# Moving the key products and the gain of an HGRN2 stage from VectorE and ScalarE to GpSimd

## The chip, the core and the metric

The kernel runs on one core of one Trainium2 chip. The metric is the device time of one launch in microseconds (us). A core has five engines with instruction streams of their own: PE (TensorE, matrix products), DVE (VectorE), ACT (ScalarE), POOL (GpSimd) and SP (SyncE, which here only starts transfers). They meet only at semaphores.

## The reference

A program of two blocks on 256 rows of width 1024: a first block with three attention branches and a feed-forward part, then two layers, one with an HGRN2 mixer and a feed-forward part, one with differential attention and a mixture of eight experts. The change touches the HGRN2 mixer alone:

```python
def hgrn2_mixer(h, w_in, lb_logits, norm_g, w_out, layer):
    q, f, i, g = jnp.split(h @ w_in, 4, axis=-1)
    lb = jnp.cumsum(jax.nn.softmax(lb_logits, axis=0), axis=0)[layer]
    forget = lb + (1.0 - lb) * jax.nn.sigmoid(f)
    log_f = jnp.log(forget)
    k = 1.0 - forget
    q = jax.nn.silu(q)
    v = i
    ...
        cum = jnp.cumsum(lf, axis=2)
        rel = jnp.where(tri, cum[:, :, :, None, :] - cum[:, :, None, :, :], -jnp.inf)
        scores = jnp.einsum('bhtd,bhsd,bhtsd->bhts', qc, kc, jnp.exp(rel))
    ...
    o = rms_norm_2(o, norm_g) * jax.nn.sigmoid(g).reshape(b, s, nh, dk)
    return o.reshape(b, s, D_MODEL) @ w_out
```

There are 8 heads of width 128. `norm_g` (`hg_norm_g_2`) is one gain for each of the 128 columns of a head, the same for all heads.

## The kernel before

All matrix products of the projections are done with each operand split into a high and a low part (three matmuls for one). Weights come by SP's queue into a ring; ACT writes the high part of each quarter of a weight tile (L1255, "a piece"), DVE the low part (L1864, the split), and PE uses them. Both run a few pieces ahead of PE and may write over a piece only when PE has used it.

The HGRN2 scores are computed by levels. Level i, from 0 to 8, pairs queries in the second half of each stretch of 2b positions with keys in its first half, b = 128, 64, 32, 16, 8, 4, 2, 1, and level 8 is the diagonal. For each level:

- DVE subtracts the cumulated log at the middle of each stretch (`level_differences`, L2244 or L2247, result in DD);
- ACT takes the exponentials of both halves into EE (`level_exps`, L1542 and L1543), and may do so only when queries and keys of the level before are done, since EE is written over;
- DVE multiplies the second halves of the queries QQ into QS (`level_queries`, L2257) and the first halves of the keys KK into KS (`level_keys`, L2266), when PE has read QS and KS of the level before;
- PE computes the products of all heads (`level`, L885), 16 matmuls for level 0 and 32 for each other, when both are there;
- the result goes from PSUM into the score matrix STT: by ACT for levels 0 and 1 (`level_copy`), by DVE under a mask from level 2 on (`level_place`, L2276, four predicated copies).

There is one QS, one KS, one EE and one DD. The order is written out by hand: the levels lie between the quarters q of four projections, hg0, hg1 (the gate), hv0, hv1 (the values), level i behind the quarter that LEVEL_AT gives, so that PE has two quarters of a projection between two levels:

```python
                    if (n, q) in LEVEL_AT:
                        i = LEVEL_AT[n, q]
                        if i + 1 < 8:
                            level_differences(i + 1)
                        if i >= 2:
                            level_place(i)
                        if i + 1 < 8:
                            level_queries(i + 1)
                            level_keys(i + 1)
```

The gate is tanh(x/2) on ACT (L1563) and then 0.5 t + 0.5 on DVE (`gate_rows2`, L2283), into GN, rows by columns. After the levels the scores are multiplied by the values, ACT squares the result, DVE sums (L2318), POOL takes the inverse root (L2758), DVE multiplies by the root (L2327) and by the gate (L2330). PE turns the result into columns (`columns("ho", ...)`), and there the gain is a number for each partition: ACT writes the high part times VT's column V_HN (L1273) and DVE the low part with the same column (L1892). That column comes by a 0.5 KB load of SP's into VS and a turn on PE, with all other column vectors.

POOL sets buffers to zero ahead of the stage, computes KK (L2848) and has no other work between 527 and 617 us. In other stages it multiplies and adds rows of 128x512 (L2780, L2782, L2838).

Of the kernel before, what the change touches and what calls it, by code (L numbers as in the profile page):

```python
# [54 lines left out]
V_MIX, V_MEM, V_FFN, V_LNG, V_LNB, V_QF, V_KF, V_QC, V_KC, V_LB, V_HN = 0, 8, 16, 24, 56, 88, 89, 90, 91, 92, 116  # L55
# [67 lines left out]
def build(nc, I, table, out):  # L123
    ctx = ExitStack()
    with ctx:
# [18 lines left out]
        NG = sb("NG", [128, 128])  # L144
# [65 lines left out]
        s_gth, s_gg, s_osq, s_od = (sem(n) for n in ("s_gth", "s_gg", "s_osq", "s_od"))  # L210
# [8 lines left out]
        T = {}  # L219
# [118 lines left out]
        VECTORS = [(V_FFN, "g_ffn", 8), (V_LNG, "ln_g_2", 32), (V_LNB, "ln_b_2", 32), (V_LB, "hg_lb_2", 24), (V_HN, "hg_norm_g_2", 1), (V_QC, "g_q_mem", 1), (V_KC, "g_k_mem", 1)]  # L338
# [80 lines left out]
        def pe_program(e):  # L419
# [262 lines left out]
            pe.wait_ge(s_vec, 16 * 11)  # L682
# [554 lines left out]
        def act_program(e):  # L1237
# [26 lines left out]
            def column_halves(name, scale=None, tts=(0, 1), halves=(0, 1), one=None):  # L1264
                for tt in tts:
                    a.wait_ge(*T["xfree", name, tt])
                    for half in halves:
                        j = 2 * tt + half
                        a.wait_ge(*banks.full["cols", name, j])
                        ps = PS[banks_of[name][j]].rearrange("p (a n) -> p a n", a=4)  # L1270
                        x = XH[:, 4 * half:4 * half + 4, 128 * tt:128 * tt + 128]
                        if one is not None:
                            e.activation(x, ps, ACT.Copy, scale=VT[:, one:one + 1]).then_inc(s_colh, 1)  # L1273
                        elif scale is None:
# [324 lines left out]
            column_halves("ho", one=V_HN)  # L1599
# [253 lines left out]
        def dve_program(e):  # L1853
# [29 lines left out]
            def column_lows(name, scale=None, tts=(0, 1), halves=(0, 1), one=None):  # L1883
                for tt in tts:
                    for half in halves:
# [5 lines left out]
                        if one is not None:  # L1891
                            e.scalar_tensor_tensor(out=l2, in0=ps, scalar=VT[:, one:one + 1], in1=h2.bitcast(F32), op0=ALU.mult, op1=ALU.subtract).then_inc(s_cols, 1)  # L1892
                        elif scale is None:
# [32 lines left out]
            def unit_rows(n):  # L1926
                nh = HEADS[n]
                for tt in range(2):
# [55 lines left out]
            def forget(stage):  # L1984
                if stage == 0:
# [3 lines left out]
                    v.wait_ge(s_bc, 16 * 7)  # L1989
# [80 lines left out]
            v.wait_ge(s_bc, 16 * 7)  # L2070
# [188 lines left out]
            def level_keys(i):  # L2259
                ev, kv, ksv = (flat(x).rearrange("p (y x b) -> p y x b", x=2, b=LEVELS[i]) for x in (EE, KK, KS))  # L2260
                v.wait_ge(s_ee, i + 1)
                v.wait_ge(s_set, 3)
                v.wait_ge(s_kk, 1)
                if i:
                    v.wait_ge(*T["level", i - 1])
                e.tensor_tensor(ksv[:, :, 0, :], kv[:, :, 0, :], ev[:, :, 0, :], ALU.mult).then_inc(s_ks, 1)  # L2266

# [31 lines left out]
            level_keys(0)  # L2299
            for n in ("hg0", "hg1", "hv0", "hv1"):  # L2300
                for q in range(4):
# [3 lines left out]
                    if (n, q) in LEVEL_AT:  # L2305
# [15 lines left out]
            v.wait_ge(s_gg, 4)  # L2321
# [9 lines left out]
            column_lows("ho", one=V_HN)  # L2331
# [24 lines left out]
            t_ng = v.step(e.tensor_scalar(NG[:, :], NG[:, :], 1.0 - LAM_INIT, None, ALU.mult))  # L2356
# [36 lines left out]
            def da_rows(g):  # L2393
                r = root(("da", g))
                for q in range(2):
# [5 lines left out]
                    e.tensor_tensor(ov, ov, NG[:, :].unsqueeze(1).to_broadcast([128, 4, 128]), ALU.mult).then_inc(s_doo, 1)  # L2401
# [351 lines left out]
        def pool_program(e):  # L2753
# [46 lines left out]
            for dst, name, n in ((GM[:, 0, :], "g_q_moba", 64), (GM[:, 1, :], "g_k_moba", 64),  # L2800
                                 (NG[:, :], "da_norm_g_2", 128), (LAMB[:, :], "da_lam_2", 256), (BFG[:, :], "b_forget", 8)):
# [44 lines left out]
            e.memset(KS, 0.0).then_inc(s_set, 1)  # L2846
# [3 lines left out]
            e.memset(QS, 0.0).then_inc(s_q0, 1)  # L2850

            for tt in range(2):
                inverse_root(("hg", tt))
# [258 lines left out]
```

## Time and profile before

| | |
|---|---|
| time, three runs | 1947.41, 1947.96 (median), 1948.62 us |
| the profiled execution | 1947.41 us, its span 1945.6 us |
| granted TensorE clock, mean | 0.982 |
| the levels of HGRN2 | 538 to 614 us |

Times in the views are counted from the start of the span. A row of a view in order of time gives start, duration, engine, line, operation, output and inputs, shapes, how many instructions were merged, and in brackets how long the engine had idled and what ended that. Recorded durations overlap a little from one instruction to the next, so the start-to-start distance is the better price of an instruction in a row without gaps.

### The profile page before, as it was taken

To read this page: it belongs to the slowest core of one execution; us is meant where nothing else is said; L and a number is where in the kernel's file an instruction comes from. 1 tells how busy PE (TensorE), PEld (TensorE's weight loads), DVE (VectorE), ACT (ScalarE), POOL (GpSimd) and SP (SyncE) were. 2 spreads that over 40 slices of the span, in tenths; PEclk is the share of its full clock that TensorE was granted. 3 is DMA by queue.
4 is the path that set the end of the run, shared out by engine and by line. 5 is a ranking of instruction groups with operands and counts; after the bars stand their busy time and mean duration, and the time that the engine had idled before them with its cause. 6 is when DMAs were issued, how large, how long until landed. Compare 5 with 4: busy or idle time off the path is not lost.

```text
span 1945.6 us, 22484 instructions
## 1 busy us (share of the span) xinstructions
PE 1858.4 (96%) x9212; PEld 1542.6 (79%) x9212; DVE 1481.6 (76%) x1434; ACT 1217.8 (63%) x1253; POOL 135.2 (7%) x115
## 2 busy tenths in 40 slices
PE   7999999999999999989969999999999999999997
PEld 6888878888987788867758887888778887788875
DVE  5655566444689654477769899998999989998897
ACT  6555546333654443335537788877887778777784
POOL 2501100000200300042120000000000000000000
PEclk9999999999999999989979999999999999999999
DMA  8434445545432564443348999999999999999994
GB/s 294 167 130 143 152 174 181 178 168 195 156 128 89 193 215 176 149 151 130 132 152 314 377 356 412 408 393 361 374 408 413 376 358 399 409 389 367 364 410 177
DMA packets 154783, 511.56 MB, mean 263 GB/s; under 512 B 4431, under 2 KB 8898, under 8 KB 140338
## 3 DMA queue, kind: packets, MB, share of 16 engines
q1 hardware_dynamic: 152674, 504.53, 68.7%
q0 software_dynamic: 1392, 4.53, 0.7%
q8 instruction: 75, 1.23, 0.3%
q10 hardware_dynamic: 608, 0.99, 0.1%
q14 instruction: 34, 0.28, 0.0%
HBM read 508.98 MB, written 1.05 MB: 262 GB/s over the span
## 4 chain that ended last, share of the span: by engine, by line
PE 76%; DVE 14%; DMA 4%; ACT 3%; issue 2%; POOL 0%; ACTq 0%; SPq 0%; DVEq 0%; POOLq 0%
PE PS L437 21%; PE PS L439 21%; PE PS L438 21%; DVE WLB L1864 5%; DVE WLX L1864 4%; DMA ring<-in_moe_w_down 4%; PE PS L885 2%; PE PS L1104 1%; PE PS L1105 1%; ACT WHB L1255 1%; PE PS L1037 1%; PE PS L1035 1%; PE PS L582 1%; PE PS L1082 1%; PE PS L1086 1%
## 5 line engine op out<-in xcount | busy, mean ns | idle before, releaser
L1255 ACT ACTIVATE WHB<-ring 128x2048 fp32r<-128x2048 f32 (+1 forms) x344 | 534.1, 1562 | 332.6 <-PE PS L439 299.8
L1864 DVE TENSOR_TENSOR WLB<-ring,WHB 128x2048 fp32r<-128x2048 f32 (+1 forms) x344 | 636.5, 1865 | 122.1 <-ACT WHB L1255 121.5
L1864 DVE TENSOR_TENSOR WLX<-ring,WHX 128x2048 fp32r<-128x2048 f32 (+1 forms) x216 | 468.3, 2192 | 50.3 <-ACT WHX L1255 50.2
L1255 ACT ACTIVATE WHX<-ring 128x2048 fp32r<-128x2048 f32 (+1 forms) x216 | 393.7, 1838 | 157.1 <-PE PS L439 136.1
L437 PE MATMUL PS<-WHB,XH 128*128 128x512 f32 (+1 forms) x640 | 258.3, 404 | 15.2 <-DVE XL L1915 6.8
L439 PE MATMUL PS<-WHB,XL 128*128 128x512 f32 (+1 forms) x640 | 251.2, 392 | 0.0
L438 PE MATMUL PS<-WLB,XH 128*128 128x512 f32 (+1 forms) x640 | 250.3, 391 | 0.0
L437 PEld LDWEIGHTS PS<-WHB,XH 128*128 128x128 f32 x640 | 122.8, 192 | 43.9 <-issue 11.7
L439 PEld LDWEIGHTS PS<-WHB,XL 128*128 128x128 f32 x640 | 122.4, 191 | 26.0
L438 PEld LDWEIGHTS PS<-WLB,XH 128*128 128x128 f32 x640 | 122.9, 192 | 23.4
L2758 POOL TENSOR_TENSOR SM<-SM,MH 128x8 f32<-128x8 f32 (+3 forms) x28 | 38.2, 1368 | 1443.6 <-DVE SM L1877 1443.5
L437 PE MATMUL PS<-WHX,XH 128*128 128x512 f32 (+1 forms) x240 | 92.0, 383 | 4.7 <-DVE WLX L1864 4.7
L1058 PE MATMUL PS<-WHB,EH 128*128 128x512 f32 x224 | 90.8, 406 | 3.0 <-DVE WLB L1864 2.1
L439 PE MATMUL PS<-WHX,XL 128*128 128x512 f32 (+1 forms) x240 | 91.0, 379 | 0.0
L438 PE MATMUL PS<-WLX,XH 128*128 128x512 f32 (+1 forms) x240 | 90.8, 378 | 0.0
L1058 PE MATMUL PS<-WHX,EH 128*128 128x512 f32 x224 | 89.9, 401 | 0.4
L437 PE MATMUL PS<-WHX,EH 128*128 128x512 f32 x224 | 89.2, 398 | 0.0
L437 PE MATMUL PS<-WHB,EH 128*128 128x512 f32 x224 | 88.5, 395 | 0.0
L437 PE MATMUL PS<-WHB,HTH 128*128 128x512 f32 x224 | 87.9, 392 | 0.0
L439 PE MATMUL PS<-WHB,EL 128*128 128x512 f32 x224 | 87.7, 392 | 0.0
L438 PE MATMUL PS<-WLB,EH 128*128 128x512 f32 x224 | 87.7, 391 | 0.0
L439 PE MATMUL PS<-WHX,EL 128*128 128x512 f32 x224 | 87.6, 391 | 0.0
(416 smaller groups left out, 3471.9 us busy)
## 6 DMA issues: line engine op xcount, KB each, us to landing
ring<-in_moe_w_gate SPq DMA_DIRECT2D x56, 2048.0 KB, 10.3
ring<-in_moe_w_up SPq DMA_DIRECT2D x56, 2048.0 KB, 10.8
ring<-in_moe_w_down SPq DMA_DIRECT2D x56, 2048.0 KB, 10.6
ring<-in_w_in SPq DMA_DIRECT2D x13, 2048.0 KB, 8.0
ring<-in_hg_w_in SPq DMA_DIRECT2D x8, 2048.0 KB, 8.4
ring<-in_da_w_in SPq DMA_DIRECT2D x6, 2048.0 KB, 8.1
ring<-in_w_gate SPq DMA_DIRECT2D x5, 2048.0 KB, 7.8
ring<-in_w_up SPq DMA_DIRECT2D x5, 2048.0 KB, 7.8
```

What stands on the lines that cost most here:

```text
L437: e.matmul(o, xh, wh, start=start, stop=False)
L438: e.matmul(o, xh, wl, start=False, stop=False)
L439: return e.matmul(o, xl, wh, start=False, stop=stop)
L582: t = e.matmul(PS[4 + q][:, dv * h:dv * h + dv], PTBUF[a][h % 2][:, 128 * j:128 * j + 128], VR[VK[a]][:, k, dv * h:dv * h + dv], start=(k ...
L885: t = e.matmul(PS[b][:, 128 * j:128 * j + 128], a_k[:, h, 128 * s_t:128 * s_t + 128], a_q[:, h, 128 * t_t:128 * t_t + 128], start=True, st ...
L1035: t = e.matmul(PS[b][:, at_:at_ + 64], src[:, tt, 128 * d:128 * d + 128], PO[:, tt, 0:64], start=(tt == 0), stop=(tt == 1))
L1037: t = e.matmul(PS[b][:, 128 * j:128 * j + CAP], src[:, tt, 128 * d:128 * d + 128], PO[:, tt, :], start=(tt == 0), stop=(tt == 1))
L1058: e.matmul(PS[b][:, :], EH[:, kt, :], wh, start=(kt == 0), stop=False)
L1082: t = e.matmul(PS[6][:, at_:at_ + 64], inner(src, j), CT2[:, 128:192], start=True, stop=True)
L1255: e.activation(hi, src, ACT.Copy).then_inc(s_hi, 1)
L1864: e.tensor_tensor(lo, src, hi.bitcast(F32), ALU.subtract).then_inc(s_lo, 1)
L2758: e.tensor_tensor(RR[name], RV[name], MH[:, 0:RR[name].shape[1]], ALU.pow).then_inc(s_rs, 1)
```

## The change

The eight key products (`level_keys`) go from DVE's program to POOL's, with the same operands and order. The gain of the output norm is no longer applied to columns behind the turn. It is loaded as a row, spread over all partitions, by POOL's queue into a second half of NG, and POOL multiplies it into the gate GN, in four products of 128x512 (`gain_gates`): two behind the keys of level 3 and two behind those of level 5. The ACT copies and DVE subtractions on the turned columns lose their scale column; the DVE product with the gate waits for the four gain products.

```diff
-VECTORS = [..., (V_HN, "hg_norm_g_2", 1), ...]          # SP queue, column vectors
-            pe.wait_ge(s_vec, 16 * 11)
+            pe.wait_ge(s_vec, 16 * 10)
...
-            column_halves("ho", one=V_HN)
+            column_halves("ho")
-            column_lows("ho", one=V_HN)
+            column_lows("ho")
...
-                        v.wait_ge(s_bc, 16 * 7)
+                        v.wait_ge(s_bc, 16 * 8)
...
             level_queries(0)
-            level_keys(0)
...
                             level_queries(i + 1)
-                            level_keys(i + 1)
...
-            v.wait_ge(s_gg, 4)
+            v.wait_ge(s_ggp, 4)
...
# POOL's program
-            for dst, name, n in (..., (NG[:, :], "da_norm_g_2", 128), ...
+            for dst, name, n in (..., (NG[:, 0, :], "hg_norm_g_2", 128), (NG[:, 1, :], "da_norm_g_2", 128), ...
...
+            def level_keys(i):
+                ev, kv, ksv = (flat(x).rearrange("p (y x b) -> p y x b", x=2, b=LEVELS[i]) for x in (EE, KK, KS))
+                p.wait_ge(s_ee, i + 1)
+                if i:
+                    p.wait_ge(*T["level", i - 1])
+                e.tensor_tensor(ksv[:, :, 0, :], kv[:, :, 0, :], ev[:, :, 0, :], ALU.mult).then_inc(s_ks, 1)
+
+            def gain_gates(n):
+                c = int(n[2])
+                p.wait_ge(s_bc, 16 * 8)
+                for tt in range(2):
+                    g4 = GN[:, tt, 512 * c:512 * c + 512].rearrange("p (h d) -> p h d", h=4)
+                    p.wait_ge(s_gg, 2 * c + tt + 1)
+                    e.tensor_tensor(g4, g4, NG[:, 0, :].unsqueeze(1).to_broadcast([128, 4, 128]), ALU.mult).then_inc(s_ggp, 1)
+
+            level_keys(0)
+            for i in range(1, 8):
+                level_keys(i)
+                if i == 3:
+                    gain_gates("hg0")
+                if i == 5:
+                    gain_gates("hg1")
```

## Rows read from the trace of the kernel before

**Rows 1.** The page: PE's busy time, share of the span, instructions.

```profile
PE 1858.4 (96%) x9212; PEld 1542.6 (79%) x9212; DVE 1481.6 (76%) x1434; ACT 1217.8 (63%) x1253; POOL 135.2 (7%) x115
```

**Rows 2.** PE in order of time: levels 1, 3, 5, 6 and 7.

```profile
550.05 3.81 PE L885 MATMUL PS<-AR 128*128 128x128 f32 x32 [1.17 <-issue]
...
568.87 3.81 PE L885 MATMUL PS<-AR 128*128 128x128 f32 x32 [0.41 <-issue]
...
588.02 3.81 PE L885 MATMUL PS<-AR 128*128 128x128 f32 x32 [0.61 <-issue]
...
597.26 2.92 PE L885 MATMUL PS<-AR 128*128 128x128 f32 x24
...
606.51 7.38 PE L885 MATMUL PS<-AR 128*128 128x128 f32 x64
```

**Rows 3.** DVE in order of time, from level 0 to level 7.

```profile
538.68 1.23 DVE L2257 TENSOR_TENSOR AR<-AR 128x1024 f32<-128x1024 f32 x1 [1.40 <-ACT AR L1526]
...
543.23 2.29 DVE L2247 TENSOR_TENSOR AR<-AR 128x2048 f32<-128x2048 f32 x1
547.59 1.23 DVE L2257 TENSOR_TENSOR AR<-AR 128x1024 f32<-128x1024 f32 x1 [2.07 <-ACT AR L1543]
...
549.87 2.35 DVE L1864 TENSOR_TENSOR WLB<-ring,WHB 128x1024 fp32r<-128x1024 f32 x2
...
568.68 2.36 DVE L1864 TENSOR_TENSOR WLB<-ring,WHB 128x1024 fp32r<-128x1024 f32 x2
570.95 2.30 DVE L2247 TENSOR_TENSOR AR<-AR 128x2048 f32<-128x2048 f32 x1
573.15 2.62 DVE L2276 COPY_PREDICATED AR<-LEVM,PS 128x512 f32<-128x512 uint16 x4
575.66 1.21 DVE L2257 TENSOR_TENSOR AR<-AR 128x1024 f32<-128x1024 f32 x1
576.78 1.22 DVE L2266 TENSOR_TENSOR AR<-AR 128x1024 f32<-128x1024 f32 x1
577.92 1.22 DVE L1864 TENSOR_TENSOR WLB<-ring,WHB 128x1024 fp32r<-128x1024 f32 x1
579.05 0.76 DVE L2283 TENSOR_SCALAR BC<-BC 128x512 f32<-128x512 f32 x2
...
606.30 2.38 DVE L1864 TENSOR_TENSOR WLB<-ring,WHB 128x1024 fp32r<-128x1024 f32 x2
```

**Rows 4.** POOL in order of time, in stages other than HGRN2.

```profile
71.42 0.32 POOL L2771 TENSOR_TENSOR AR<-AR,CT 128x64 f32<-128x64 f32 x1 [1.85 <-DVE AR L1942]
...
231.49 6.99 POOL L2838 TENSOR_TENSOR AR<-AR 128x512 f32<-128x512 f32 x4 [51.56 <-DVE AR L2016]
...
657.89 1.29 POOL L2780 TENSOR_TENSOR H<-LZ,BC 128x512 f32<-128x512 f32 x1
...
852.63 2.21 POOL L2782 TENSOR_TENSOR H<-H,BC 128x512 f32<-128x512 f32 x1
```

**Rows 5.** DVE in order of time beside those POOL operations.

```profile
230.72 2.58 DVE L2016 TENSOR_TENSOR AR<-PS,AR 128x512 f32<-128x512 f32 x4
...
852.50 5.66 DVE L1864 TENSOR_TENSOR WLB<-ring,WHB 128x1024 fp32r<-128x1024 f32 x3
```

**Rows 6.** ACT in order of time: exponentials, a square, a scaled copy.

```profile
534.03 1.04 ACT L1543 ACTIVATE AR<-AR 128x1024 f32<-128x1024 f32 x1
...
545.55 1.06 ACT L1542 ACTIVATE AR<-AR 128x1024 f32<-128x1024 f32 x1 [0.24 <-DVE AR L2247]
...
619.55 0.60 ACT L1598 ACTIVATE AR<-PS 128x512 f32<-128x512 f32 x1 [1.19 <-PE PS L923]
...
627.59 0.69 ACT L1273 ACTIVATE XH<-PS,VT 128x512 fp32r<-128x512 f32 x1 [0.64 <-PE PS L457]
```

**Rows 7.** Windows: length; PE, PEld, DVE, ACT, POOL busy; PE clock; DMA share, GB/s.

```profile
40.00:44.00 4.00, 1.95 (x9) 1.14 (x8) 3.32 (x13) 3.75 (x15) 0.00 (x0) 1.00 0.18 69
...
620.00:627.00 7.00, 3.46 (x15) 2.42 (x16) 6.65 (x12) 2.21 (x4) 1.98 (x2) 0.77 0.01 2
```

More of the change, by code:

```diff
@@ L53 @@
 C_END = 2112
-V_MIX, V_MEM, V_FFN, V_LNG, V_LNB, V_QF, V_KF, V_QC, V_KC, V_LB, V_HN = 0, 8, 16, 24, 56, 88, 89, 90, 91, 92, 116
+V_MIX, V_MEM, V_FFN, V_LNG, V_LNB, V_QF, V_KF, V_QC, V_KC, V_LB = 0, 8, 16, 24, 56, 88, 89, 90, 91, 92
 def constant_table():
@@ L143, in build @@
         BC = sb("BC", [128, 2, D])
-        NG = sb("NG", [128, 128])
+        NG = sb("NG", [128, 2, 128])
         GM = sb("GM", [128, 2, 64])
@@ L209, in build @@
         s_ed, s_ee, s_qs, s_ks, s_lv, s_stt, s_vv = (sem(n) for n in ("s_ed", "s_ee", "s_qs", "s_ks", "s_lv", "s_stt", "s_vv"))
-        s_gth, s_gg, s_osq, s_od = (sem(n) for n in ("s_gth", "s_gg", "s_osq", "s_od"))
+        s_gth, s_gg, s_ggp, s_osq, s_od = (sem(n) for n in ("s_gth", "s_gg", "s_ggp", "s_osq", "s_od"))
         s_lam, s_lme, s_rx, s_ru, s_mix, s_dsq, s_doo = (sem(n) for n in ("s_lam", "s_lme", "s_rx", "s_ru", "s_mix", "s_dsq", "s_doo"))
@@ L1262, in piece_done, with column_halves @@
                 split_to(done[0] + 3)
-            def column_halves(name, scale=None, tts=(0, 1), halves=(0, 1), one=None):
+            def column_halves(name, scale=None, tts=(0, 1), halves=(0, 1)):
                 for tt in tts:
@@ L1271, in column_halves @@
                         x = XH[:, 4 * half:4 * half + 4, 128 * tt:128 * tt + 128]
-                        if one is not None:
-                            e.activation(x, ps, ACT.Copy, scale=VT[:, one:one + 1]).then_inc(s_colh, 1)
-                        elif scale is None:
+                        if scale is None:
                             e.activation(x, ps, ACT.Copy).then_inc(s_colh, 1)
@@ L1881, in root, with column_lows @@
                 return RR[name]
-            def column_lows(name, scale=None, tts=(0, 1), halves=(0, 1), one=None):
+            def column_lows(name, scale=None, tts=(0, 1), halves=(0, 1)):
                 for tt in tts:
@@ L1890, in column_lows @@
                         h2, l2 = XH[xs], XL[xs]
-                        if one is not None:
-                            e.scalar_tensor_tensor(out=l2, in0=ps, scalar=VT[:, one:one + 1], in1=h2.bitcast(F32), op0=ALU.mult, op1=ALU.subtract).then_inc(s_cols, 1)
-                        elif scale is None:
+                        if scale is None:
                             e.tensor_tensor(l2, ps, h2.bitcast(F32), ALU.subtract).then_inc(s_cols, 1)
@@ L1988, in forget @@
                     v.wait_ge(*banks.full["fg", 1])
-                    v.wait_ge(s_bc, 16 * 7)
+                    v.wait_ge(s_bc, 16 * 8)
                     e.tensor_tensor(FZ, PS[3][:, 256:272].rearrange("p (a h) -> p a h", a=2), BFG[:, :].unsqueeze(1).to_broadcast([128, 2, 8]), ALU.add).then_inc(banks.out["fg", 1][0], 1)
@@ L2069, in dve_program @@
             first_layer(ITEMS[2:4])
-            v.wait_ge(s_bc, 16 * 7)
+            v.wait_ge(s_bc, 16 * 8)
             for i, w in enumerate((WFG, WRT)):
@@ L2257, in level_queries @@
                 e.tensor_tensor(qsv[:, :, 1, :], qv[:, :, 1, :], ev[:, :, 1, :], ALU.mult).then_inc(s_qs, 1)
[L2259 to L2266, printed above, removed]
             def level_place(i):
@@ L2355, in dve_program @@
             t_nl = v.step(e.tensor_scalar(NL, NL, -LAM_INIT, None, ALU.add))
-            t_ng = v.step(e.tensor_scalar(NG[:, :], NG[:, :], 1.0 - LAM_INIT, None, ALU.mult))
+            t_ng = v.step(e.tensor_scalar(NG[:, 1, :], NG[:, 1, :], 1.0 - LAM_INIT, None, ALU.mult))
             def rope_rows(n, i):
@@ L2400, in da_rows @@
                     v.wait_ge(*t_ng)
-                    e.tensor_tensor(ov, ov, NG[:, :].unsqueeze(1).to_broadcast([128, 4, 128]), ALU.mult).then_inc(s_doo, 1)
+                    e.tensor_tensor(ov, ov, NG[:, 1, :].unsqueeze(1).to_broadcast([128, 4, 128]), ALU.mult).then_inc(s_doo, 1)
             def da_mix(h):
@@ L2799, in pool_program @@
                 inverse_root(("kc", tt))
-            for dst, name, n in ((GM[:, 0, :], "g_q_moba", 64), (GM[:, 1, :], "g_k_moba", 64),
-                                 (NG[:, :], "da_norm_g_2", 128), (LAMB[:, :], "da_lam_2", 256), (BFG[:, :], "b_forget", 8)):
+            for dst, name, n in ((GM[:, 0, :], "g_q_moba", 64), (GM[:, 1, :], "g_k_moba", 64), (NG[:, 0, :], "hg_norm_g_2", 128),
+                                 (NG[:, 1, :], "da_norm_g_2", 128), (LAMB[:, :], "da_lam_2", 256), (BFG[:, :], "b_forget", 8)):
                 e.dma_start(dst, spread(I[name], n)).then_inc(s_bc, 16)
@@ L2845, in pool_program @@
             e.memset(STT, 0.0).then_inc(s_set, 1)
-            e.memset(KS, 0.0).then_inc(s_set, 1)
+            t_ks = p.step(e.memset(KS, 0.0))
             p.wait_ge(s_sg, 8)
@@ L2850, in pool_program @@
             e.memset(QS, 0.0).then_inc(s_q0, 1)
+            p.wait_ge(*t_ks)
+            p.wait_ge(s_kk, 1)
+            def level_keys(i):
[18 more added lines that the diff above has]
+                    gain_gates("hg1")
             for tt in range(2):
```

2 lines of the change are left out of this document (1 added, 1 removed).

## The prediction

> **What bounds the kernel now.** I read the busy shares first: PE is busy for 96% of the span [rows 1], so a change pays only where PE waits for another engine. I then read PE in order of time over the HGRN2 stage, from 541 to 614 us. It idles only in front of a level's block of 128x128 matmuls (L885): 1.17 us in front of level 1 at 550.05, 0.41 us in front of level 3 at 568.87, 0.61 us in front of level 5 at 588.02 [rows 2]. In front of levels 2, 4, 6 and 7 it does not wait. So the stage holds 2.2 us of PE idleness, and no rearrangement of its other engines can return more.
>
> The view of VectorE in order of time shows why those waits exist. From 558 to 608 us DVE has no gap. One cycle, from 568.68 to 577.92, is two weight splits (2.27), the differences (2.20), four predicated copies (2.51), the queries (1.12) and the keys (1.14): 9.24 us. A cycle with two gate operations (579.05) has 0.7 more [rows 3]. PE's own cycle is 9.25 us when it doesn't wait, levels 6 to 7 (597.26 to 606.51) [rows 2]. DVE and PE are level with each other: whatever lengthens the cycle of DVE, ScalarE and GpSimd beyond 9.25 us lengthens the program by as much.
>
> Call Q the moment at which queries and keys of a level are both done; PE starts the level 0.18 us later (549.87 to 550.05) if it was waiting. Q is 549.87 for level 1 and 606.30 for level 7 [rows 2, 3].
>
> **The change, part by part.**
>
> *Eight key products leave DVE.* Each is 128x1024 with both inputs in SBUF and holds DVE for 1.14 us from start to start (576.78 to 577.92) [rows 3].
>
> *Eight key products enter POOL.* POOL's product costs 0.32 us for 128x64 (71.42, in rows of 8) and 1.29 us for 128x512 (657.89) when alone [rows 4], 2.17 ns a column; for 1024 columns I get 1.29 + 512 x 2.17 ns = 2.40 us. This is an estimate from shorter rows. Rows of 4, 2 and 1 elements, which levels 5 to 7 read, no row of POOL shows.
>
> *Who waits.* The keys of level i need the exponentials of level i, which ScalarE ends 2.16 us after the differences (545.43 to 547.59, the row whose idle time ends at L1543) [rows 3]. In the present kernel the four predicated copies (2.51) cover that time. POOL could start 2.16 + 0.05 us after the differences, 0.3 us before DVE reaches the queries.
>
> *The collision.* From 852.50 us DVE ran three 128x1024 splits, each with two SBUF inputs, beside POOL products of 128x512. The three took 5.66 us, where three in a row take 1.14 + 1.14 + 1.22 = 3.50, and POOL's product at 852.63 took 2.21, where one alone takes 1.29 [rows 4, 5]. The two POOL products that ran between three splits thus held DVE for 2.16 us, 1.08 each, and I round to 1.1. They take turns, one whole instruction at a time. The price of POOL work beside a DVE operation of this kind is thus its own time less some 0.2 us (1.29 less 1.1) of start-up: 2.2 us for the keys, 1.1 for a gain. Where DVE reads PSUM and one SBUF tensor, nothing stretches: four such products from 230.72 took 2.58 us, 0.64 each, with POOL's products already running at 231.49 [rows 4, 5]. The predicated copies read PSUM and a mask, so I take them to be free of it; if they were not, the keys would start 0.3 us later in five levels: 1.5 us, in the range.
>
> The Trainium skill ("SBUF — State Buffer", section "Who interferes with whom") says that a Vector instruction with at most one SBUF input doesn't contend with GpSimd, and one with two does against a GpSimd read. By that rule the predicated copies stay free and the sum stands; without it 1.5 us are added. No row here puts a predicated copy beside POOL.
>
> *The new cycle.* Splits (2.27) and differences (2.20) and exponentials (2.16 + 0.05) come in a row, then POOL's keys (2.3 on a lane partly free) and DVE's queries (1.14) one after the other: 10.1 us against 9.24, or +0.86 for each of levels 3 to 7 = **+4.3**. The order of keys and queries does not matter, nor whether a split comes first, since DVE must do all of them before the next differences.
>
> *Levels 1 and 2* have no predicated copies; there DVE already waits for the exponentials, then needs 547.59 to 549.87 = 2.28 us [rows 3]. The new pair takes 0.05 + 2.3 + 1.14 = 3.49, **+1.21 each**. Level 0's keys need only the exponentials that start at 534.03 and run 1.04 us; POOL does them by 537.5, and what they hold up on DVE falls in the 1.40 us that it idled before 538.68 [rows 3, 6]. DVE then reaches the differences of level 1 1.14 us sooner, but the exponential at 545.55 had waited only 0.24 us for them [rows 6]: **-0.25** is left. Levels 1 and 2 together: +2.2.
>
> *Four gain products are added on POOL*, two behind the keys of level 3 and two behind those of level 5, 128x512 with both inputs in SBUF. They meet queries, splits and differences, and DVE is the bound of the cycle: 4 x 1.1 = **+4.4**. If DVE held the lane until its predicated copies, they would cost nothing.
>
> *What leaves in exchange.* The gain column goes from four ScalarE copies of 128x512, 0.69 us each; a square of the same size without a column, at 619.55, is 0.60 [rows 6]. PE waits behind one of them at a time: **-0.1**. DVE's four subtractions stay four operations: nothing. PE started level 7 0.21 us after Q (606.51 to 606.30), so it had no slack to give there [rows 2, 3].
>
> *DMAs and waits.* One 0.5 KB load leaves SP's queue, one load of a 128-wide row spread over partitions enters POOL's at about 30 us, in front of two small loads whose readers come at 68 us: nothing. The wait for seven loads becomes one for eight, and all are long landed. Nothing in the stage waits behind POOL but the roots of the output's mean squares; the squares they rest on begin after 614 us, behind all of POOL's new work. The final product now waits for the gains, which end with level 5.
>
> **Sum:** 4.3 + 2.2 + 4.4 - 0.1 = +10.8 us. The profiled execution took 1947.41 us (span 1945.6 and 1.8 around it), which is the lowest of three; the median is 1947.96. I predict 1947.4 + 10.8 = **1958.2 us**, 0.5% over the median. A change under 0.2% (3.9 us) could not be told from none.
>
> **PE's clock.** The new waits are 0.9 us in most cycles and up to 3.2 us in two. With PE busy for 1.95 of the 4 us from 40 us on, the granted clock stayed at 1.00, full speed of 2.4 GHz; with 3.46 of 7 us busy it fell to 0.77 [rows 7]. At 1.2 GHz for 3 us PE would lose 1.5 us, in cycles where it has as much to spare. I cost it at nothing and keep +1.5 as a bound.
>
> **The rivals.**
> 1. *No turn-taking.* The key product runs beside DVE and ends 2.16 + 0.05 + 2.40 us after the differences. The cycle is 4.47 + 4.6 = 9.1, under PE's 9.25; gate cycles are 9.8. PE gets back about 1 us of its 2.2, and the tail 0.1: 1946.3, not slower. It decides from a POOL hold of about 1.4 us down. Against it stand the splits at 852.50 us [rows 4, 5]; for it, that no row shows this pair of operations. 9%.
> 2. *DVE wins the lane while it has work,* and POOL's gains slide under the predicated copies. The 4.4 us go: 1953.8. Against it: from 852.50 on POOL's products got in between splits that DVE had ready [rows 4, 5]. 12%.
> 3. *Short rows are dear on POOL.* At worst levels 5 to 7 pay for each column what the 128x64 product pays with its start-up, 0.32 / 64 = 5.0 ns: 5.1 us for the keys instead of 2.4, +2.7 for each of three levels, 1966.3; half of that is 1962.2. No row decides; the POOL product in rows of 8 (71.42) costs what its size says [rows 4]. 14%, with a fall of the clock.
>
> The Trainium skill ("GPSIMD Engine Reference", section "Performance pitfalls for Q7 kernels") puts a penalty of about half on reads whose inner step is over 8 bytes. Here the longest inner step is two floats, 8 bytes, in level 7. By that rule rival 3 does not come about and the sum stands; no run here shows it yet.
>
> 4. *Something frees more than the 2.2 us that PE waits.* I see no place for it. 2%.
>
> **How the numbers follow.** The forecast, 1956 to 1961, has 63%, rival 2 12%, rival 3 and the clock 14%, rival 1 9%, rival 4 2%. The range 1952 to 1964.5 leaves out rivals 1 and 4 and the far end of 3, about 15%. Slower by over 0.2%: 89%; within 0.2%: 9%; faster: 2%.
>
> **What would show it.** Right: keys on POOL of 2.4 us alone (level 0) and 2.4 to 3.6 beside the queries; queries, or the split behind them, of 2.3 to 3.5 us where they were 1.22; PE waits of about 2 us before level 1, 0.9 to 1.5 in front of the others, about 3 in front of levels 4 and 6; level 7 starting near 617. Wrong: DVE operations that keep their 1.22 us beside POOL (rival 1); gains that run at the time of the predicated copies (rival 2); keys that lengthen from level 5 on (rival 3); the difference arising outside 538 to 620 us.

## The result and the profile after

The changed kernel took 1961.99 us, the median of 4 runs (1961.64 to 1962.94), against 1948.29 us for the kernel before on the same chip (4 runs, 1947.41 to 1948.96). The ratio is 1.0069, with a 95% interval of 1.0056 to 1.0082: slower by 11 to 16 us, where +10.8 was forecast. Its profiled execution took 1961.01 us with a span of 1959.2, which is 13.6 us more than before.

The page of the changed kernel, PE's busy time first, answers to [rows 1]:

```profile
PE 1862.3 (95%) x9212; PEld 1546.3 (79%) x9212; DVE 1493.6 (76%) x1426; ACT 1216.9 (62%) x1253; POOL 166.5 (9%) x128
```

From here on *the lane* is what VectorE and GpSimd cannot have at the same time when both read SBUF. (So these two do not meet only at semaphores, as the opening has it.) DVE's busy time rose by 12.0 us although eight of its instructions left, 1.22 us each. Its queries and splits between levels 0 and 7 became some 21 us longer in their place: they wait for the lane, and a wait inside an instruction counts as busy.

PE in order of time, levels 0 to 7, the rows that answer to [rows 2]:

```profile
543.21 1.95 PE L885 MATMUL PS<-AR 128*128 128x128 f32 x16
...
552.69 5.44 PE L885 MATMUL PS<-AR 128*128 128x128 f32 x32 [2.02 <-issue]
...
564.04 3.81 PE L885 MATMUL PS<-AR 128*128 128x128 f32 x32 [0.40 <-issue]
...
574.69 3.84 PE L885 MATMUL PS<-AR 128*128 128x128 f32 x32 [1.33 <-DVE AR L2253]
...
586.87 5.47 PE L885 MATMUL PS<-AR 128*128 128x128 f32 x32 [2.83 <-DVE AR L2253]
...
597.69 3.76 PE L885 MATMUL PS<-AR 128*128 128x128 f32 x32
...
610.42 5.47 PE L885 MATMUL PS<-AR 128*128 128x128 f32 x32 [3.46 <-DVE AR L2253]
...
621.24 6.98 PE L885 MATMUL PS<-AR 128*128 128x128 f32 x61
```

Level 0 of the kernel before in the same view:

```profile
541.42 1.95 PE L885 MATMUL PS<-AR 128*128 128x128 f32 x16
```

Level 0 to level 7 is 621.24 - 543.21 = 78.03 us. Before, it was 606.51 [rows 2] - 541.42 = 65.09. The stage explains +12.9 of the +13.6. PE now waits in front of five levels, 1, 2, 3, 4 and 6; the longest waits are 2.8 and 3.5 us, in front of levels 4 and 6, and the queries of DVE end those of levels 3, 4 and 6. The blocks of levels 1, 4 and 6 last 5.4 to 5.5 us instead of 3.8: more on this under e5.

This distance, level 0 to level 7, is my measure in all experiments. It comes from one traced execution of each kernel. In the kernel before it is 65.09, and in two variants that turned out to change nothing it is 65.12 and 65.05, while whole executions of the kernel before range from 1945.0 to 1956.8 us over the chips.

POOL in order of time, with the keys in L2844 and the gains in L2852:

```profile
536.80 2.40 POOL L2844 TENSOR_TENSOR AR<-AR 128x1024 f32<-128x1024 f32 x1 [8.54 <-ACT AR L1541]
549.19 3.40 POOL L2844 TENSOR_TENSOR AR<-AR 128x1024 f32<-128x1024 f32 x1 [9.99 <-ACT AR L1541]
...
571.15 2.40 POOL L2844 TENSOR_TENSOR AR<-AR 128x1024 f32<-128x1024 f32 x1 [7.21 <-ACT AR L1541]
573.51 4.46 POOL L2852 TENSOR_TENSOR BC<-BC,NG 128x512 f32<-128x512 f32 x2
...
606.46 2.82 POOL L2844 TENSOR_TENSOR AR<-AR 128x1024 f32<-128x1024 f32 x1 [5.57 <-ACT AR L1541]
617.13 2.87 POOL L2844 TENSOR_TENSOR AR<-AR 128x1024 f32<-128x1024 f32 x1 [7.85 <-ACT AR L1541]
```

DVE in order of time over level 3, with queries in L2253, splits in L1862, differences in L2243 and predicated copies in L2263, the operations of the cycle in [rows 3]:

```profile
568.96 2.63 DVE L2263 COPY_PREDICATED AR<-LEVM,PS 128x512 f32<-128x512 uint16 x4
571.47 3.17 DVE L2253 TENSOR_TENSOR AR<-AR 128x1024 f32<-128x1024 f32 x1
574.56 4.49 DVE L1862 TENSOR_TENSOR WLB<-ring,WHB 128x1024 fp32r<-128x1024 f32 x2
578.97 2.28 DVE L2243 TENSOR_TENSOR AR<-AR 128x2048 f32<-128x2048 f32 x1
581.18 2.62 DVE L2263 COPY_PREDICATED AR<-LEVM,PS 128x512 f32<-128x512 uint16 x4
```

The keys take 2.40 us where the lane is free, exactly the estimate. The queries (1.21 alone) become 3.17, since they wait for the keys to end, and two splits (2.36 alone) become 4.49 beside the two gains. The keys of level 3 (571.15) begin beside the last of the copies of 568.96, and neither is longer. Keys of 2-element and 1-element rows (606.46, 617.13) take 2.82 and 2.87.

### The profile page after: what moved, and what is told of

Read it like the earlier page. It is cut to its first block, busy times and chain, and to the rows that moved or that the text cites. A ratio compares the mean times of both kernels' runs of the same rounds, so it can differ in the third digit from the quotient of the medians.

```text
span 1959.2 us, 22497 instructions
## 1 busy us (share of the span) xinstructions
PE 1862.3 (95%) x9212; PEld 1546.3 (79%) x9212; DVE 1493.6 (76%) x1426; ACT 1216.9 (62%) x1253; POOL 166.5 (9%) x128
## 4 chain that ended last, share of the span: by engine, by line
PE 72%; DVE 17%; DMA 4%; ACT 3%; issue 2%; POOL 0%; SPq 0%; DVEq 0%; ACTq 0%; POOLq 0%
PE PS L437 20%; PE PS L439 20%; PE PS L438 20%; DVE WLB L1862 6%; DVE WLX L1862 4%; DMA ring<-in_moe_w_down 4%; PE PS L1104 1%; PE PS L1105 1%; ACT WHB L1255 1%; PE PS L885 1%; PE PS L1037 1%; DVE AR L2253 1%; PE PS L1035 1%; PE PS L582 1%; PE PS L1082 1%
## 5 line engine op out<-in xcount | busy, mean ns | idle before, releaser
L1862 DVE TENSOR_TENSOR WLB<-ring,WHB 128x2048 fp32r<-128x2048 f32 (+1 forms) x344 | 646.1, 1893 | 125.2 <-ACT WHB L1255 124.7
L1862 DVE TENSOR_TENSOR WLX<-ring,WHX 128x2048 fp32r<-128x2048 f32 (+1 forms) x216 | 467.9, 2190 | 49.9 <-ACT WHX L1255 49.8
## 6 DMA issues: line engine op xcount, KB each, us to landing
ring<-in_moe_w_up SPq DMA_DIRECT2D x56, 2048.0 KB, 10.9
```

The lines of the kernel that those rows point to most:

```text
L1862: e.tensor_tensor(lo, src, hi.bitcast(F32), ALU.subtract).then_inc(s_lo, 1)
```

## The experiments

Some of the twelve kernels divide the sum into its terms, the others ask how POOL and DVE share the lane and what PE's clock does. Unless told otherwise every kernel starts from the kernel before. Diffs are cut to their core.

**e1_gain_only.** The keys stay on DVE. Only the gains are on POOL, asked for when the keys of levels 3 and 5 are done.

```diff
...
+            p.wait_ge(s_ks, 4)
+            gain_gates("hg0")
+            p.wait_ge(s_ks, 6)
+            gain_gates("hg1")
```

> The gain moves to GpSimd, the keys stay on DVE; the gains run behind the keys of levels 3 and 5. Theory (POOL products and DVE operations with two SBUF inputs take turns): each gain holds DVE's splits for 1.1 us, so +4.4 us, 1952.7; the splits behind levels 3 and 5 take about 4.5 us a pair instead of 2.36. Rival (they run side by side): within 0.5 us of the kernel before.

Measured: 1949.35 us, ratio 0.9997 (0.9985 to 1.0009), 65.12 us from level 0 to level 7. The expectation missed: the gains cost nothing. The view of the gains' line gives least, median and greatest duration in ns, and POOL in order of time has the first two in one row:

```profile
L2853 POOL TENSOR_TENSOR BC<-BC,NG x4: 1301/3434/5562, 570.3 to 595.0; 128x512 f32<-128x512 f32 x4
```

```profile
570.33 6.82 POOL L2853 TENSOR_TENSOR BC<-BC,NG 128x512 f32<-128x512 f32 x2 [41.49 <-DVE AR L2262]
```

The same kernel's DVE in order of time beside the first of them:

```profile
570.16 2.35 DVE L1862 TENSOR_TENSOR WLB<-ring,WHB 128x1024 fp32r<-128x1024 f32 x2
572.43 2.29 DVE L2243 TENSOR_TENSOR AR<-AR 128x2048 f32<-128x2048 f32 x1
574.63 2.64 DVE L2272 COPY_PREDICATED AR<-LEVM,PS 128x512 f32<-128x512 uint16 x4
```

The first gain is issued at 570.33 and lasts 5.56 us. DVE's two splits and the differences keep their durations, and the gain ends 1.26 us after the copies begin, so it got its 1.3 us of work only beside them. That is rival 2, the behaviour to which I had given 12%, in an arrangement where the gains stand alone. "They take turns, one whole instruction at a time" is not a rule.

**e2_keys_only.** All eight keys are on POOL, and the gain column stays where it was.

```diff
-                            level_keys(i + 1)
...
+            for i in range(8):
+                level_keys(i)
```

> The keys move to GpSimd, the gain stays with the turned columns. Theory of turns: the changed kernel's 1962.0 less the four gains (4.4) = 1957.6; level 1 begins with a PE wait of about 2 us and its matmuls run at half the granted clock for part of it. Rival (keys beside DVE cost nothing, the loss is the gains and something upstream): 1949 or less.

Measured: 1959.44 us, ratio 1.0052 (1.0032 to 1.0072), 72.27 us from level 0 to level 7, +7.2. The slow matmuls that were expected in level 1 did not come: its block took 3.81 us, so the clock has no part in the 7.2. PE in order of time, levels 0 to 2 and the last:

```profile
543.32 1.95 PE L885 MATMUL PS<-AR 128*128 128x128 f32 x16
...
552.79 3.81 PE L885 MATMUL PS<-AR 128*128 128x128 f32 x32 [2.02 <-issue]
...
562.75 3.81 PE L885 MATMUL PS<-AR 128*128 128x128 f32 x32 [0.65 <-issue]
...
615.59 7.41 PE L885 MATMUL PS<-AR 128*128 128x128 f32 x64 [1.35 <-DVE AR L2257]
```

Against the level starts of before, the seven intervals grew by 0.84, 0.80, 0.98, 0.81, 0.85, 1.45 and 1.45 us. Levels 3 to 5 were sized at 0.86. Levels 6 and 7 cost 0.59 more each, the levels in which POOL's product lengthened from 2.38 to 2.86 us. Level 2 cost 0.80 instead of 1.21: PE had 0.25 us of slack there, which I had not taken off (its keys and queries ended at 558.78 before, and PE started at 559.21, 0.43 later and not 0.18). The other 0.16 us of that difference was not followed up.

**e3_gain_late.** The changed kernel, with all four gains behind the keys of level 7, from the first predicated copy of level 7 on.

```diff
...
-                if i == 3:
-                    gain_gates("hg0")
-                if i == 5:
-                    gain_gates("hg1")
+            p.wait_ge(*banks.out["lv", 7, 0, 0])
+            gain_gates("hg0")
+            gain_gates("hg1")
```

> The changed kernel with all four gains behind the keys of level 7, held until the first predicated copy of level 7 is done, so that they run beside predicated copies only. Theory: predicated copies (one SBUF input, one PSUM) don't take turns with POOL, the copies keep 0.64 us from start to start and the gains 1.3 us each; 1962.0 - 4.4 = 1957.6. Rival (predicated copies take turns too): the copies stretch by up to 4.4 us in all and the time stays at 1960 to 1962.

Measured: 1956.38 us, ratio 1.0032 (1.0021 to 1.0043), 73.69 us from level 0 to level 7. POOL and then DVE in order of time, at the gains:

```profile
618.05 4.97 POOL L2852 TENSOR_TENSOR BC<-BC,NG 128x512 f32<-128x512 f32 x4 [4.08 <-DVE AR L2263]
```

```profile
617.26 3.37 DVE L2263 COPY_PREDICATED AR<-LEVM,PS 128x512 f32<-128x512 uint16 x5
620.78 0.74 DVE L2263 COPY_PREDICATED AR<-LEVM,PS 128x512 f32<-128x512 uint16 x1 [0.16 <-PE PS L885]
```

Four gains take 1.24 us each beside five copies that take 3.37; in the trace of the kernel before the same five take 3.42 without POOL. So these predicated copies, which read PSUM and a mask, are not held up by POOL. Against the changed kernel, 4.34 us are gone: 2.13 between levels 3 and 4, 2.04 between levels 5 and 6. So behind the keys the gains do cost what was forecast (4.4), and in e1 they cost nothing. The blocks of levels 4 and 6, slow in the changed kernel, take 3.84 us in e3.

**e4_products_unread** and **e4_writes_unread.** Nobody waits for POOL in either. The first has a 128x1024 product of two SBUF tensors in every level, into an unused buffer, asked for at the exponentials' end. The second has writes of about the same duration in its place.

```diff
+            for i in range(8):
+                p.wait_ge(s_ee, i + 1)
...
+                t = p.step(e.tensor_tensor(spare.rearrange("p (y b) -> p y b", b=128), kv[:, :, 0, :], kv[:, :, 1, :], ALU.mult))
```

```diff
...
+                for n in (1024, 1024, 256):
+                    t = p.step(e.memset(spare[:, 0:n], 0.0))
```

> The kernel before, keys on DVE, plus eight POOL products of 128x1024 with two SBUF inputs, one beside each level's keys, whose output nobody reads and for which nobody waits. Theory of turns: a product that no one waits for costs as much as it holds DVE, 2.2 us at each of levels 1 to 7 less 0.3 where it begins under the predicated copies, less 1 us of slack: 13 us, 1961 (some 1.5 more if the granted clock falls at level 1). Rival (the loss comes from waiting for POOL's result and its semaphores): within 0.5 us of the kernel before.

> The kernel before plus, in the place of the eight unread products, eight groups of three POOL memsets (1024, 1024 and 256 columns, about 2.3 us a group) that read nothing. If the turns are about the reading of SBUF, DVE's operations keep their 1.22 and 2.29 us and the time stays within 1 us of the kernel before. If any POOL work beside DVE costs, it comes out like the unread products, 15 us or more above.

Measured: products 1970.45 us, ratio 1.0106 (1.0087 to 1.0125), 81.30 us from level 0 to level 7; writes 1948.63, ratio 0.9997 (0.9985 to 1.0009), 65.05. DVE in order of time at level 1, with the products and then with the writes:

```profile
548.68 1.22 DVE L2257 TENSOR_TENSOR AR<-AR 128x1024 f32<-128x1024 f32 x1 [2.07 <-ACT AR L1543]
549.82 3.37 DVE L2266 TENSOR_TENSOR AR<-AR 128x1024 f32<-128x1024 f32 x1
```

```profile
547.85 1.22 DVE L2257 TENSOR_TENSOR AR<-AR 128x1024 f32<-128x1024 f32 x1 [2.07 <-ACT AR L1543]
548.99 1.22 DVE L2266 TENSOR_TENSOR AR<-AR 128x1024 f32<-128x1024 f32 x1
```

Work on POOL is not what costs; reading SBUF on POOL is. A product holds DVE up by 3.37 - 1.22 = 2.15 us, as sized (2.2). The expectation of 13 us was still too low: it took PE's slack and the copies off, and the trace shows nearly the full hold in each level. The ratio stands for 17 to 24 us, more than the stage's 16.2; the traced execution, 1965.22 us, was the fastest of four, and where the others lost more isn't known. Level 0's product fell into an idle time of DVE; the seven others give 7 x 2.15 = 15.1 of the 16.2 us in the stage, and the remaining 1.1 lie behind level 1, where PE's block took 5.44 us (e5 has that cause). The Trainium skill ("SBUF — State Buffer", section "Who interferes with whom") says both things, that a Vector instruction with two SBUF inputs contends with GpSimd's reads and not with its writes, and the trace agrees.

**e5_pe_filled.** The changed kernel, with matmuls nobody reads where PE would wait for levels 1, 4 and 6, so that it is busy through those waits.

```diff
+            FILL = {1: 9, 4: 12, 6: 14}
...
+                if i in FILL:
+                    room(6)
+                    for _ in range(FILL[i]):
+                        e.matmul(PS[6][:, :], XH[:, 0, 0:128], XH[:, 0:2, :], start=True, stop=True)
```

> The changed kernel with matmuls of no use (9, 12 and 14 of 128x512 into a bank that the level rewrites) in the waits of PE before levels 1, 4 and 6. Theory (the wait of 2 us lets the granted clock fall, and the slow matmuls of level 1 delay ScalarE's copies and so the next exponentials): level 1's 32 matmuls take 3.8 us and not 5.4, the distance from level 1 to level 2 is 10.0 us and not 11.4, the clock stays at 1.00 over the stage, and the time falls by 1.4 us; levels 4 and 6 give nothing, since DVE sets their cycle. Rival (the slow matmuls have another cause): 5.4 us stays.

Measured: 1960.79 us, ratio 1.0064 (1.0043 to 1.0085), 76.64 us from level 0 to level 7 against 78.03. In the time the 1.4 us can't be told from none. Windows of the changed kernel, and then of e5, over level 1 (length; PE, PEld, DVE, ACT, POOL busy; PE clock; DMA share, GB/s):

```profile
554.00:559.00 5.00, 5.00 (x29) 4.82 (x29) 3.01 (x2) 1.89 (x5) 0.00 (x0) 0.70 0.00 0
```

```profile
554.00:559.00 5.00, 5.00 (x27) 4.22 (x27) 2.93 (x3) 3.73 (x5) 1.66 (x1) 1.00 0.00 0
```

ACT in order of time, at level 1's first and last copy and the next exponential, in the changed kernel:

```profile
553.91 0.38 ACT L1554 ACTIVATE AR<-PS 64x256 f32<-64x256 f32 x1 [1.67 <-PE PS L885]
...
558.16 0.38 ACT L1554 ACTIVATE AR<-PS 64x256 f32<-64x256 f32 x1 [0.51 <-PE PS L885]
558.44 1.04 ACT L1540 ACTIVATE AR<-AR 128x1024 f32<-128x1024 f32 x1
```

After a wait of 2.02 us PE's granted clock falls to 1.2 GHz for part of the block (mean 0.70 of 2.4 GHz in this window), and the block at 552.69 takes 5.44 us instead of 3.81. ScalarE's four copies follow that block and stand before the exponentials in its queue, so the exponentials of level 2 start 1.4 us late, and everything behind them is as much later. At levels 4 and 6 the slow blocks (5.47) hide behind DVE: the intervals 4 to 5 and 6 to 7, 10.82 us each, are 10.76 and 10.69 in e5. The fall costs 1.4 us at one place of three. It does not follow from the wait alone. In front of level 1, e2 and e11 waited 2.02 us and e9 2.01, and all three kept 3.81 us; e3 waited 2.02 and e8 1.95, and their blocks took 5.44.

**e6_gain_on_the_copies_end.** As e1, but the gains are asked for during the predicated copies of levels 2 and 4, before DVE's row of queries, keys and splits.

```diff
-            p.wait_ge(s_ks, 4)
+            p.wait_ge(*banks.out["lv", 2, 1, 0])
...
-            p.wait_ge(s_ks, 6)
+            p.wait_ge(*banks.out["lv", 4, 1, 0])
```

> As e1 (keys on DVE, gain on POOL), which cost nothing since its first gain waited 4.3 us for DVE to leave a row of operations with two SBUF inputs. Here the same gains start after the third predicated copy of levels 2 and 4, while the lane is free. Theory (a POOL operation that is there before DVE's next one is issued gets the lane, and keeps taking every second turn as long as it has more to do): queries are held 0.8 us and keys 1.1 us in two cycles, +3.8 us to the stage from level 0 to level 7. Rival (DVE goes first whenever it has work, so that the turns of the changed kernel are special to it): +1.6 us or less.

Measured: 1953.57 us, ratio 1.0022 (1.0012 to 1.0033), 70.10 us from level 0 to level 7, +5.0 where 3.8 was expected. POOL in order of time, and then PE at level 5:

```profile
565.65 3.51 POOL L2853 TENSOR_TENSOR BC<-BC,NG 128x512 f32<-128x512 f32 x2 [38.62 <-DVE AR L2272]
586.63 3.51 POOL L2853 TENSOR_TENSOR BC<-BC,NG 128x512 f32<-128x512 f32 x2 [17.47 <-DVE AR L2272]
```

```profile
591.32 5.44 PE L885 MATMUL PS<-AR 128*128 128x128 f32 x32 [2.43 <-issue]
```

The four products that were free in e1 cost here. Two last 3.51 us and not 6.82: they get in between DVE's instructions. In the edit only the moment of the request differs. The 5.0 us are not all theirs. The intervals in which they hold DVE, 2 to 3 and 4 to 5, grew by 1.81 and 1.82 us (9.66 to 11.47 and 9.91 to 11.73): 3.6. After its wait of 2.43 us PE's granted clock fell in level 5's block (0.50 from 593 to 595 us), which took 5.44 us; PE did not wait for level 6, and the interval 5 to 6 grew by 1.55, of which 0.16 came back in the next. By these intervals the holds are 3.6 us and the slow clock 1.4.

**e8_request_later** and **e11_row_after_a_pause.** What decides who gets in? In both, an unread POOL product of 128x512 is asked for in every level when the queries end, later by a POOL write of n columns. In e8 n is 0, 128, ... 896 for levels 0 to 7. In e11 n is 896, 1984, 640, 0, 0, 0, 512, 896, and DVE pauses before the queries of levels 5 to 7.

```diff
+            for i in range(8):
+                p.wait_ge(s_qs, i + 1)
...
+                    t = p.step(e.memset(blank[:, 0:128 * i], 0.0))
...
+                t = p.step(e.tensor_tensor(spare[:, 0:512], k2[:, 0:512], k2[:, 512:1024], ALU.mult))
```

```diff
+                            if i >= 4:
+                                v.wait_ge(s_hand, i - 3)
                             level_queries(i + 1)
```

> The kernel before, with an unread POOL product of 128x512 (two SBUF inputs, plain contiguous rows) in every level, asked for when the level's queries end, and behind a POOL write of 0, 128, 256, ... 896 columns in levels 0 to 7, so that its request comes at eight different moments of DVE's row of keys, splits and differences (about 0.2, then 0.5 to 1.3 us after the keys' start). Level 0 to level 7 is 65.1 us in the kernel before. Theory 1, turns at every instruction whenever POOL asks: each product takes 1.3 to 2.4 us, and a level's DVE row is 1.1 us longer: 65.1 + 7 x 1.1 - 2.2 (PE's slack is gone already, so only what DVE had idle at levels 1 and 2 is absorbed) = about 70.5. Theory 2, DVE keeps the lane through a row of such instructions unless POOL asks within some 0.15 us of an instruction's start: most products last 3 to 6 us, until DVE's predicated copies or its idle time begin, all DVE operations keep 1.22 and 2.29, and level 0 to level 7 is 65 to 66 us; a level whose request happens to fall at the start of an instruction pays 1.1.

> As e8 (the kernel before with an unread POOL product of 128x512 in every level, asked for when the queries end), with the moments and the history of DVE's row exchanged: writes of 896, 1984 and 640 columns delay the request in levels 0, 1 and 2, whose rows begin after an idle time of DVE; no delay in levels 3 and 4, whose rows follow the predicated copies without a gap; and in levels 5, 6 and 7 DVE waits for a POOL write before the queries, so that its row begins after a pause of some 0.4 us, with the request not delayed, 512 and 896 columns late. Theory 1, the history decides (a row that begins after an idle time lets POOL in at the next instruction, one that runs on without a gap keeps it out until copies or idle time): products of 1.3 to 2.4 us in levels 0, 1, 2, 5, 6, 7 and of 5 to 6.5 us in levels 3 and 4. Theory 2, the moment of the request in the row decides (in by 0.65 us after an instruction's start, kept out later): products of 1.3 to 2.4 us in levels 3, 4, 5, 6, and about 5 us in levels 0, 1 and 7 (3.5 us in level 1). In either case a product that gets in holds DVE up for 1.1 us. Level 0 to level 7: 65.1 + 3 x 0.4 for the pauses, + 1.1 for each product that gets in behind the second level.

Measured, one execution each: e8 1954.97 us and 68.33 from level 0 to level 7; e11 1960.52 and 74.61. POOL in order of time, e8 at levels 0, 2, 3, 4 and 6, then e11 at levels 0, 1, 3, 4 and 7:

```profile
541.85 2.13 POOL L2860 TENSOR_TENSOR YL<-AR 128x512 fp32r<-128x512 f32 x1 [13.35 <-DVE AR L2257]
...
562.46 1.77 POOL L2860 TENSOR_TENSOR YL<-AR 128x512 fp32r<-128x512 f32 x1
...
573.58 6.16 POOL L2860 TENSOR_TENSOR YL<-AR 128x512 fp32r<-128x512 f32 x1
...
582.93 6.72 POOL L2860 TENSOR_TENSOR YL<-AR 128x512 fp32r<-128x512 f32 x1
...
602.33 5.83 POOL L2860 TENSOR_TENSOR YL<-AR 128x512 fp32r<-128x512 f32 x1
```

```profile
542.17 2.36 POOL L2867 TENSOR_TENSOR YL<-AR 128x512 fp32r<-128x512 f32 x1
...
553.22 1.28 POOL L2867 TENSOR_TENSOR YL<-AR 128x512 fp32r<-128x512 f32 x1
...
572.23 2.13 POOL L2867 TENSOR_TENSOR YL<-AR 128x512 fp32r<-128x512 f32 x1 [8.87 <-DVE AR L2257]
...
582.56 2.12 POOL L2867 TENSOR_TENSOR YL<-AR 128x512 fp32r<-128x512 f32 x1 [8.21 <-DVE AR L2257]
...
617.23 1.28 POOL L2867 TENSOR_TENSOR YL<-AR 128x512 fp32r<-128x512 f32 x1
```

In e8 the products of levels 0 to 2 got in at the next instruction and those of levels 3 to 7 were kept out for the whole row. In e11 all eight got in. Each that got in held DVE up by 1.1 us (two splits, 2.35 alone, take 3.43 or 3.44): e8 65.09 + 3 x 1.1 = 68.4 against 68.33; e11 65.09 + 7 x 1.1 + 1.8 of pauses = 74.6 against 74.61 (the eighth holds a split that ends behind level 7's start). For e8 the sum comes out in part by luck: level 1's block ran slow there, after which DVE idled 2.33 us instead of 2.07, and level 0 started some 0.3 us later behind its keys than before. The price is settled by the lengths of the splits. Neither theory of who gets in held. Theory 1 expected levels 3 and 4 of e11 to be kept out, and they got in. Theory 2 expected levels 0, 1 and 7 of e11, asked for 1.07 to 2.20 us after the keys' start, to be kept out, and they got in.

**e9_keys_0_to_2** and **e10_keys_6_and_7.** Only these levels' keys on POOL.

```diff
-                            level_keys(i + 1)
+                            if i + 1 not in (6, 7):
+                                level_keys(i + 1)
...
+            for i in (6, 7):
+                level_keys(i)
```

> The kernel before with the keys of levels 0, 1 and 2 alone on POOL. Theory: levels 1 and 2 cost 1.21 us each, level 0 gives back 0.25: +2.2 us, and +1.4 more if PE's clock falls in level 1; level 0 to level 7 is 67.3 us (68.7 with the clock) against 65.1, DVE beside a key product 2.3 to 3.4 us. Rival (no turns): 64 to 65.1. In the time +1.1 to +3.6 us, near what can be told from none.

> The kernel before with the keys of levels 6 and 7 alone on POOL (rows of 2 elements and of 1). Theory: 0.86 us for each and 0.45 more for each because POOL's product of such short rows takes 2.85 us and not 2.40: level 0 to level 7 is 65.1 + 2.6 = 67.7 us. If short rows cost nothing on the path: 66.8. POOL's products 2.8 to 2.9 us, DVE's queries 3.7 to 3.9. In the time +2 to +3 us.

Measured: e9 1951.14 us, ratio 1.0015 (1.0005 to 1.0024), 66.93 us from level 0 to level 7, +1.8 (the 2.2 of the sum less level 2's slack leaves 1.95). e10 1958.17 us, ratio 1.0051 (1.0034 to 1.0068), 72.78 us, +7.7 where 2.6 was expected. POOL, and then DVE and PE in order of time, in e10 at level 6:

```profile
595.22 8.32 POOL L2860 TENSOR_TENSOR AR<-AR 128x1024 f32<-128x1024 f32 x1 [67.47 <-ACT AR L1543]
```

```profile
595.18 1.24 DVE L2257 TENSOR_TENSOR AR<-AR 128x1024 f32<-128x1024 f32 x1
596.31 2.38 DVE L1864 TENSOR_TENSOR WLB<-ring,WHB 128x1024 fp32r<-128x1024 f32 x2
598.58 2.31 DVE L2247 TENSOR_TENSOR AR<-AR 128x2048 f32<-128x2048 f32 x1
```

```profile
603.64 5.62 PE L885 MATMUL PS<-AR 128*128 128x128 f32 x32 [5.91 <-issue]
```

The key product asked for the lane 0.04 us after DVE's queries had taken it and stayed out until DVE ran dry at 600.9, four instructions later. PE waited 5.91 us. In the changed kernel the products of levels 6 and 7 were issued 0.15 and 0.12 us before the queries, during the copies, and went first. Being kept out is free only when nobody waits for the product.

**e7_copies_as_cover.** The version that the findings point to: POOL gets work only where DVE is idle or copies, and nobody waits for it soon. That is level 0's keys, the gates' multiply-add beside the copies of levels 2 and 3, and one gain beside the copies of each of levels 4 to 7.

```diff
-                    if q == 0 and n in ("hg1", "hv0"):
-                        gate_rows2("hg0" if n == "hg1" else "hg1")
...
+            p.wait_ge(s_ed, 4)
+            gates_here("hg0")
...
+            for k in range(4):
+                p.wait_ge(*((s_ed, 6 + k) if k < 3 else banks.out["lv", 7, 0, 0]))
...
+                e.tensor_tensor(g4, g4, NG[:, 0, :].unsqueeze(1).to_broadcast([128, 4, 128]), ALU.mult).then_inc(s_ggp, 1)
```

> A version that uses the covers found: keys of level 0 alone on POOL, the gate's 0.5 t + 0.5 on POOL beside the predicated copies of levels 2 and 3, one gain product beside those of each of levels 4 to 7, the rest on DVE. Theory: DVE's cycles of 9.9 us become 9.25, PE's waits before levels 3 and 5 go (1.0 us) and level 1 begins 0.25 us sooner; level 0 to level 7 takes 63.9 us and not 65.1; in the time -1.2 us, less than can be told from none. Rival (POOL beside the copies costs turns after all): 66 us or more.

Measured: 1948.98 us, ratio 0.9994 (0.9982 to 1.0006). In the stage it is 63.55 us against 65.09, and PE's waits in front of levels 3 and 5 are gone. That is 1.5 of the 2.2 us that the profile of before set as the bound; PE still waits 0.94 us in front of level 1. In the whole time it can't be told from none.

## Why the prediction was right, and where its sum was off

*The total.* The median rose by 13.7 us (1948.29 to 1961.99) where 10.8 were forecast. It lies in the range, but 1 us above the band of 1956 to 1961 that I had given 63%, in the part set down for short rows and the clock. Both came, each in part: short rows 1.2 us, the clock 1.4.

*The bound.* Right. No arrangement of the stage returned more than 1.5 us, and whatever lengthened DVE's cycle lengthened the stage.

*Keys, +4.3 and +2.2 (6.5).* Right in mechanism. e2 measures 7.2: short rows cost 0.59 more in each of levels 6 and 7, and level 2 cost 0.4 less. Rival 3 was right that short rows are dearer, and wrong in its size (2.7 a level) and in level 5, whose 4-element rows cost nothing (2.38 us). By the short rows the queries of levels 6 and 7 took 3.76 and 3.83 us, above the 3.5 that I had named.

*Gains, +4.4.* Right in size: 4.3 between the changed kernel and e3. Wrong in its reason, so the size is in part luck: the turns that I read off [rows 4, 5] are one of two behaviours. The changed kernel's gains follow a key product that already had the lane, and there they took turns; e1 shows the other behaviour. That following a key product is what lets them in is not shown by an experiment of its own.

*PE's clock, costed at nothing.* Mis-sized: 1.4 us. The step that failed is "in cycles where it has as much to spare". That holds for levels 4 and 6. In level 1 ScalarE's copies, which hang on the block's end, stand in front of the exponentials. That levels 4 and 6 lost nothing needed waits there as long as the slow blocks: in e6, level 5's slow block had no such wait behind it and cost 1.4 us.

*The sum in the stage.* 7.2 of keys (e2), 4.3 of gains, 1.4 of the clock (e3 against e2, 73.69 - 72.27) = 12.9, the 12.9 measured. Predicted were 10.9. "Level 7 starting near 617" became 621.24: 2.0 from this sum, 1.8 from the later start of level 0.

*Outside the stage.* The span grew by 0.7 us more: level 0 started 1.8 us later than before and 1.1 came back behind level 7. The start of level 0 varies between 541.10 and 543.54 over the fourteen traces of this case, and e3, which has all of the change upstream, has it at 541.43. So the 1.8 need not be the change's. Of the 1.1 behind level 7 only the scaled copy's gain (0.1) was forecast, and no run here singled out the rest.

*Left open.* What decides whether POOL gets in between two of DVE's instructions. Four expectations were wrong by it (e1, e8, e10, e11). In the traces a product that POOL issues right behind another one or beside predicated copies always had its turn (the changed kernel, e2, e3, e4_products, e6). Of the products asked for in the middle of a row of DVE's, in e1 and in e8 to e11, 13 got in (e8 three, e9 two, e11 eight) and 8 were kept out (e1 two, e8 five, e10 one). The moment doesn't sort them. A pause does in one direction: all eleven in a row that DVE had begun after an idle time got in, and so did ten more of the same kind, the products of levels 1 and 2 in the changed kernel, e2, e3, e4_products and e5. Of the ten in rows that ran on from the copies without a gap, only two got in (levels 3 and 4 of e11). The nearest pair is e9 and e10. A key product asked for the lane 0.04 us after the queries had begun: at 547.87 in e9, after 2.98 us of idle time, and it took 3.39 us; at 595.22 in e10, without a gap, and it took 8.32. What let the two of e11 in stays open.

## What to carry to other kernels

Before moving work to GpSimd, find out what both engines read: here a GpSimd product that got in beside VectorE instructions with two SBUF inputs cost VectorE its own duration less some 0.2 us, and beside predicated copies from PSUM, or if it only wrote, nothing. Put only work there that nobody waits for soon, because it may be kept out for the length of VectorE's row; of the requests made here in rows that followed a pause of VectorE's, none was. Where VectorE and TensorE are level with each other, work out first how much TensorE waits at all (here 2.2 us in a stage of 65), since that is the most that unloading VectorE can return there. A wait that is added can cost more than itself, when the clock falls in the block behind it (1.4 us more in e6 and in the changed kernel).

## What the runs showed of the hardware that was not expected

- A GpSimd product issued 0.04 us after VectorE's began waited through four VectorE instructions, 5.7 us, although there is a boundary between each two (e10). Requests of the same kind got in at the next boundary 13 times in e8, e9 and e11. The Trainium skill ("SBUF — State Buffer", section "SBUF: two separate sides") lets whichever starts first have the port pair for the whole instruction; the runs here add that it can be for the whole row.
- GpSimd's 128x1024 key product takes 2.35 to 2.41 us in rows of 4 elements and more, and 2.82 to 2.88 in rows of 2 and of 1, where it did not wait (the changed kernel, e2, e3, e5, e10).
- With waits of 2.01 and 2.02 us in front of level 1, TensorE kept its full clock in e2, e9 and e11. It fell from it in the changed kernel and e3 (2.02) and in e8 (1.95), where the 3.81 us block took 5.44. In front of level 3 of e6 it kept it after 2.22 us. In the changed kernel it was still full for the first 0.5 us of the block, from 552.69, and at half from 554 to 557 us.
